# Reading the moving operand of the feed-forwards in alternating runs of its two halves

## The reference, cut to what matters

```python
def swiglu(x, w13, w2):
    a, b = jnp.split(x @ w13, 2, axis=-1)
    return (jax.nn.silu(a) * b) @ w2

def swiglu_half(x, g, w_gate, w_up, w_down):
    h = rms_norm(x, g)
    return (jax.nn.silu(h @ w_gate) * (h @ w_up)) @ w_down
```

## Time and profile before

| | |
|---|---|
| median of three runs | 1663.0 us (1661.54 to 1664.1) |
| span of the profiled execution, first to last instruction | 1659.3 us |
| own time of the profiled execution | not listed apart; the median is 3.7 us above its span |
| TensorE busy | 1609.1 us (97%) |
| VectorE busy | 1127.4 us (68%) |
| ScalarE busy | 942.3 us (57%) |
| DMA | 283.93 MB, mean 171 GB/s |

### The profile page before, as it was taken

How to read it: one execution, slowest core, us unless ns; L and a number is a source line. 1 busy time by engine, 2 the same in 40 slices (tenths; PEclk the granted TensorE clock), 3 DMA queues, 4 the chain that set the end, 5 groups by cost and what they waited for, 6 DMA issues and landing times.

```text
span 1659.3 us, 24819 instructions
## 1 busy us (share of the span) xinstructions
PE 1609.1 (97%) x9079; PEld 1365.8 (82%) x9079; DVE 1127.4 (68%) x1801; ACT 942.3 (57%) x1529; POOL 117.2 (7%) x172
## 2 busy tenths in 40 slices
PE   7999999999899999999999889999999999999999
PEld 7887888888688887888888678888888888678887
DVE  5955766687676668766768467667766666667665
ACT  5555655567665555555566565555655565665554
POOL 0602000000000000000003310000000001510000
PEclk9999999999999999999999999999999999899999
DMA  9332455583245654556664026656465675026653
GB/s 340 115 127 102 153 189 191 184 284 131 101 159 189 205 175 152 191 190 198 239 208 153 1 92 213 209 170 229 152 200 179 216 245 178 1 91 214 206 173 102
DMA packets 216787, 283.93 MB, mean 171 GB/s; under 512 B 8328, under 2 KB 152712, under 8 KB 216712
## 3 DMA queue, kind: packets, MB, share of 16 engines
q1 hardware_dynamic: 216330, 282.72, 51.1%
q10 hardware_dynamic: 382, 0.20, 0.0%
HBM read 281.81 MB, written 1.09 MB: 170 GB/s over the span
## 4 chain that ended last, share of the span: by engine, by line
PE 57%; DVE 3%; ACT 1%; POOL 0%; issue 0%; ACTq 0%; DVEq 0%
PE banks L1033 19%; PE banks L1034 10%; PE banks L792 7%; PE banks L793 7%; PE banks L794 7%; PE banks L1378 1%; PE banks L1391 1%; PE banks L1411 1%; PE banks L3017 0%; PE banks L247 0%; POOL normed L2561 0%; PE banks L2600 0%; DVE ring L379 0%; DVE gains_and_squares L1475 0%; PE banks L2988 0%
## 5 line engine op out<-in xcount | busy, mean ns | idle before, releaser
L1033 PE MATMUL banks<-act_both,ring_kept 128*128 128x512 f32 x1056 | 365.1, 391 | 4.1 <-DVE act_both L659 2.1
L1033 PE MATMUL banks<-act_both,ring 128*128 128x512 f32 x1056 | 363.8, 390 | 0.3 <-DVE ring L379 0.3
L1034 PE MATMUL banks<-act_both,ring_kept 128*128 128x256 f32 x1056 | 292.0, 276 | 0.0
L1034 PE MATMUL banks<-act_both,ring 128*128 128x256 f32 x1056 | 291.8, 276 | 0.0
L1033 PEld LDWEIGHTS banks<-act_both,ring_kept 128*128 128x128 f32 x1056 | 198.2, 188 | 48.3 <-issue 3.9
L1033 PEld LDWEIGHTS banks<-act_both,ring 128*128 128x128 f32 x1056 | 198.3, 188 | 42.5 <-DVE ring L379 1.0
L1138 ACT ACTIVATE normed<-banks 128x512 f32<-128x512 f32 x132 | 78.7, 596 | 253.9 <-PE banks L1034 253.9
L1034 PEld LDWEIGHTS banks<-act_both,ring_kept 128*128 128x128 f32 x1056 | 198.3, 188 | 2.2
L1034 PEld LDWEIGHTS banks<-act_both,ring 128*128 128x128 f32 x1056 | 198.3, 188 | 2.0
L793 PE MATMUL banks<-ffn_down_lo,ffn_hidden_both 128*128 128x512 f32 x504 | 197.6, 392 | 0.0
L792 PE MATMUL banks<-ffn_down_hi,ffn_hidden_both 128*128 128x512 f32 x504 | 197.6, 392 | 0.0
(11 more groups left out here) (412 smaller groups left out, 2766.7 us busy)
## 6 DMA issues: line engine op xcount, KB each, us to landing
weight_slots<-in_ffn_w SPq DMA_DIRECT2D x44, 1024.0 KB, 6.5
weight_slots<-in_ffn_w_gate SPq DMA_DIRECT2D x44, 1024.0 KB, 5.4
weight_slots<-in_ffn_w_up SPq DMA_DIRECT2D x44, 1024.0 KB, 8.0
weight_slots<-in_ffn_w_down SPq DMA_DIRECT2D x88, 512.0 KB, 8.4
weight_slots<-in_ffn_w SPq DMA_DIRECT2D x44, 512.0 KB, 8.3
weight_slots<-in_ev_w_in SPq DMA_DIRECT2D x6, 2048.0 KB, 13.5
weight_slots<-in_od_w_in SPq DMA_DIRECT2D x5, 2048.0 KB, 11.1
weight_slots<-in_ab_w_in SPq DMA_DIRECT2D x4, 2048.0 KB, 9.0
```

The costliest lines, as they stand in the source:

```text
L1033: pe.matmul(bank, k.hi(n)[:, q, :], k.act_both[:, q], start=q == 0, stop=False, skip_group_check=True)
L1034: return pe.matmul(bank[:, 0:S], k.lo(n)[:, q, :], k.act_hi[:, q, :], start=False, stop=q == KD - 1, skip_group_check=True)
```

## The change

A table gives each feed-forward a run length e. In the three kinds of matmul with 512 columns (L1033, and L792 to L794 as called from `down_bank`) the moving operand is no longer read from column 0 to 511. It is seen as two halves of 256 columns and read in runs of e columns, one run of the left half, then the run at the same place of the right half, and so on. The output bank is seen through the same view, so each result goes to the column where it went before. The matmuls of 256 columns (L1034) are unchanged, and so is the number, order and size of all instructions, tiles and waits. A 512-column matmul then has 512 / e runs: 32 in ffn0, 16 in ffn1, 8 in ffn2, 4 in ffn3, 64 in ffn4 and 128 in ffn5.

```diff
@@ -34,6 +34,7 @@
 LEAD = 16
+RUN = dict(ffn0=16, ffn1=32, ffn2=64, ffn3=128, ffn4=8, ffn5=4)
 FFN_LEAD = 0
@@ -983,6 +984,11 @@
+    def in_runs(ap):
+        if len(ap.shape) == 2:
+            return ap.rearrange("p (u c e) -> p c u e", u=2, e=RUN[name])
+        return ap.rearrange("p u (c e) -> p c u e", e=RUN[name])
+
@@ -1030,7 +1036,8 @@
-                pe.matmul(bank, k.hi(n)[:, q, :], k.act_both[:, q], start=q == 0, stop=False, skip_group_check=True)
+                pe.matmul(in_runs(bank), k.hi(n)[:, q, :], in_runs(k.act_both[:, q]), start=q == 0, stop=False,
+                          skip_group_check=True)
@@ -1048,7 +1055,8 @@
-                return split_products(pe, ps[:, 2 * t + h, :], (hh[:, c], hl[:, c]), (wh[:, h, :], wl[:, h, :]), start, stop,
+                return split_products(pe, in_runs(ps[:, 2 * t + h, :]), (hh[:, c], hl[:, c]),
+                                      (in_runs(wh[:, h, :]), in_runs(wl[:, h, :])), start, stop,
                                       skip_group_check=True)
```

## The result

The changed kernel takes 1701.6 us (median of four runs, 1700.79 to 1702.51), the kernel before 1662.27 us beside it (four runs, 1661.05 to 1664.1): a ratio of 1.0236, 95% interval 1.0224 to 1.0247. It is slower by 39 us. The forecast was no change; the time lies inside the range.

A forecast was written before the change was run, and what follows sets the result against it. TensorE's matmuls were taken to bound the kernel, gapless in the six feed-forwards. The only term, order of columns, was put at zero between -49.5 and +65 us: 1659.3 + 0, plus 3.7 outside the span, 1663.0 us; range 1620 to 1706.

The forecast's parts named there:

- What bounds the kernel: Six feed-forwards: TensorE busy without a gap, about 181 us each, some 1085 us together, so each nanosecond per matmul counts.
- I take zero for this term: Extra cost of run starts in 3696 matmuls of 512 columns: up to 65 us at 0.42 ns a start, set to zero.
- Short runs open stretches anew: Runs under 16 columns reopen stretches: 8.2 us in ffn4, 24.8 us in ffn5, together +33 us, 1696 us; chance 0.18.
- The matmuls no longer settle: All six feed-forwards: 1 KB jumps keep streams unsettled, 9 ns per 512 columns, 4.5 per 256; +37 us, 1700 us; chance 0.15.
- Each jump costs: Every run start takes a step in SBUF or bank: +65 us or more, 1728 us, ffn5 worst; chance 0.12.
- The halves relieve each other: Alternating halves give a place read too soon time: 1613.5 us, or 1638 us in three of six lengths; chance 0.25.
- The loss per 512 columns: Ascending matmuls taken as 13.4 ns slower than 213.3 ns at 2.4 GHz; freeing it all would gain 49.5 us.
- runs of 4 columns might be free: ffn5: four 4-byte values fill one 16-byte SBUF line, so by the skill's rule the shortest runs cost nothing.

## Why the prediction failed

- **What bounds the kernel** held: TensorE grew by the loss, the others waited more, and a nanosecond on a matmul counted with its number (15.3 us from the distances, 15.2 from the stretch, in ffn5).
- **The step that failed** is "I take zero for this term: ... the loss goes with the number of columns and with nothing else that I can see, and that is how a fixed rate looks". All the rows behind it, and the earlier trace rows, were ascending reads, so they could not show an order. The prediction says so itself ("Whether it depends on the order of the columns, no row shows") and then put the term at zero all the same. A distance of 227 ns is what the ascending order gives, no rate of the supply: all other orders but one give 231 to 535 ns. In its place stand 0 for runs of 64 and 128, and for a down matmul 8.0, 11.3, 14.3 and 22.0 ns for runs of 32, 16, 8 and 4.
- **Short runs open stretches anew** came near in time (1696 against 1701.6 us) and not in place: it had nothing in ffn0 and ffn1, which pay 7.2 and 5.3 us, 8.2 us in ffn4, which pays 10.9, and 24.8 us in ffn5, which pays 15.2. Its unit, the length of a run, is refuted by the free runs of 8 with ascending places.
- **The matmuls no longer settle** named +37 us and 4.5 ns on the 256-column matmuls, and 38.6 us and 4 to 6 ns were measured. But it wanted the same in all six, and two pay nothing; its reason, the distance to the weights, does not move the down matmuls with runs of 16 (239.8 to 240.2 ns). Its 118 ns for 256 columns was no property of the first projection: the same matmuls, which the change leaves alone, take 113.3 ns at the same place of the changed kernel's trace. It is right in part: the 256-column matmuls, and the gate product after a down product in runs of 16, pay without being changed.
- **Each jump costs** had 32, 16, 8, 4, 64, 128 as proportions; 7.2, 5.3, 0, 0, 10.9, 15.2 are none, and 32 and 64 jumps were free.
- **The halves relieve each other** fell too. The remark set down against it, that the halves "may well be the same place", was what decided: they are, as any multiple of 64 columns is. With it the prediction could have asked which run lengths take the read out of its ascending order of addresses. But the 512 bytes that it had are 128 columns, and by them runs of 64, which are free, would have been costly too; that the period is 64 columns only the runs showed.
- **The range** holds the measured time by luck: it reached up to 1706 us for the short runs and the unsettled matmuls, and neither has the costs in the right feed-forwards.
- The loss per 512 columns was taken as 13.4 ns; by the earlier trace rows it is 226.9 - 213.3 = 13.6, and the most that could be gained 50.3 us. Nothing turns on it.
- That results in runs might cost was in the jumps rival, and is not so.
- That runs of 4 columns might be free came out both ways: 250.7 ns in ffn5, 227.2 where each run lies in the next place. Below 4 columns there is a step in either order: 283 to 534 ns from 4 to 2 columns by turns in one place, 227 to 269 from 4 to 1 with the places by turns. By the Trainium skill (SBUF — State Buffer, Specifications) lines have 16 bytes and want two hits for full bandwidth. Four columns are such a line, and the step lies there; but two columns by turns have two hits on a line and take 534 ns, no less than one column, so two hits are not enough in that run. The cost of the order, paid with whole lines, is not in it.

## To carry to other kernels

When a rate looks fixed, ask whether the rows could have shown it to vary: here each row read in one order. Before a moving operand of 4-byte columns is permuted or interleaved, work out its addresses modulo 64 columns; as long as the read goes through them in ascending order its jumps and the order of the results are free here, and in the other orders with runs of 4 columns and more a matmul paid 1 to 24%, but for one (places by turns every 4 columns), where only the 256-column matmuls beside it paid. Keep weights at a multiple of 64 columns from the moving operand.

## What was not expected of the hardware

- A moving read of this type has a period of 64 columns (256 bytes): weights at distances of 16 and 80 and of 48 and 112 columns give the same times, and so do halves 192 and 256 columns apart. A period of 32 is excluded: a distance of 32 costs 3 ns, one of 64 nothing.
- The ascending read at the best distance, about 227 ns for 512 columns in gate and up and 228.7 in down products, was not beaten by any of more than 40 orders by the time of the feed-forward; the one order with a faster down matmul (227.2 ns) had 119.8 ns for 256 columns and a stretch 1.2 us longer. The 213.3 ns of 2.4 GHz was not reached.
- Two columns by turns among rows of one place take 534 ns, 2.3 times the ascending read, and one column by turns no more.
- Results in runs of 4 to 128 columns cost nothing to 0.1 ns a matmul.
